# The gated delta rule of a two-layer decoder trunk: chunks of 128 tokens for chunks of 64

## The reference, cut to what matters

```python
def chunk_gated_delta_rule(q, k, v, g, beta):      # DN_CHUNK = 64
    q, k, v, g, beta = (chunks(t) for t in (q, k, v, g, beta))
    gc = jnp.cumsum(g, axis=-1)
    decay = jnp.exp(jnp.where(incl, gc[..., :, None] - gc[..., None, :], -jnp.inf))
    k_beta = k * beta[..., None]
    lower = jnp.where(strict, einsum(k_beta, k) * decay, 0.0)
    rhs = concatenate([v * beta[..., None], k_beta * jnp.exp(gc)[..., None]])
    u, w = triangular_solve(lower + eye(C), rhs)
    qk = einsum(q, k) * decay
    # scan over chunks, with a state of 128 x 128 per head:
    v_new = u - w @ state
    o = (q * exp(gc)) @ state + qk @ v_new
    state = state * exp(g_last) + (k * exp(g_last - gc)).T @ v_new
```

## Time and profile before

| | |
|---|---|
| median of 3 runs | 783.01 us (782.78 to 783.46) |
| the profiled execution | 782.49 us, span 780.5 us |
| TensorE, matmuls | 761.1 us busy, 98% of the span, 4506 records |
| VectorE | 581.5 us, 75% |
| ScalarE | 476.4 us, 61% |
| GpSimd | 169.9 us, 22% |
| memory reads | 122.06 MB, 158 GB/s over the span |

### The profile page before, as it was taken

How to read it: one execution, slowest core, us unless ns; L and a number is a source line. 1 busy time by engine, 2 the same in 40 slices (tenths; PEclk the granted TensorE clock), 3 DMA queues, 4 the chain that set the end, 5 groups by cost and what they waited for, 6 DMA issues and landing times.

```text
span 780.5 us, 12179 instructions
## 1 busy us (share of the span) xinstructions
PE 761.1 (98%) x4506; PEld 656.9 (84%) x4506; DVE 581.5 (75%) x846; ACT 476.4 (61%) x1073; POOL 169.9 (22%) x187
## 2 busy tenths in 40 slices
PE   7999999998999999999999999999999998999998
PEld 6999888887878788888899998888778787888886
DVE  6687878978788677666656886899795975867763
ACT  6869476677685744354457776765866657433451
POOL 1255105204031012321023511231030300126100
PEclk9999999999999999999999999999999999999999
DMA  8666455454645346455566563655356453455551
GB/s 247 207 194 200 159 142 155 136 162 135 165 136 187 109 135 189 140 184 176 149 196 182 158 193 104 182 153 171 111 153 171 136 186 112 145 179 162 172 179 55
DMA packets 73041, 124.97 MB, mean 160 GB/s; under 512 B 9757, under 2 KB 17047, under 8 KB 72983
## 3 DMA queue, kind: packets, MB, share of 16 engines
q1 hardware_dynamic: 72560, 124.13, 52.2%
q10 hardware_dynamic: 423, 0.06, 0.1%
HBM read 122.06 MB, written 1.05 MB: 158 GB/s over the span
## 4 chain that ended last, share of the span: by engine, by line
PE 76%; DVE 12%; ACT 7%; issue 3%; POOL 1%; DMA 0%; ACTq 0%; POOLq 0%
PE bank L787 19%; PE bank L789 19%; PE bank L788 19%; DVE w_lo L1464 3%; PE bank L769 3%; PE bank L771 3%; PE bank L770 3%; ACT at L1399 2%; ACT w_hi L1130 2%; PE bank L817 1%; PE bank L874 1%; ACT at L1196 1%; DVE gate L1818 1%; PE bank L927 1%; DVE at L1819 1%
## 5 line engine op out<-in xcount | busy, mean ns | idle before, releaser
L1464 DVE TENSOR_TENSOR w_lo<-raw,w_hi 128x1024 fp32r<-128x1024 f32 (+4 forms) x240 | 286.9, 1223 | 96.9 <-ACT w_hi L1130 94.5
L1130 ACT ACTIVATE w_hi<-raw 128x1024 fp32r<-128x1024 f32 (+4 forms) x239 | 235.8, 1017 | 96.1 <-PE bank L789 75.0
L787 PE MATMUL bank<-w_hi,hT 128*128 128x512 f32 (+2 forms) x704 | 277.6, 394 | 5.8 <-DVE mixed L1483 3.2
L789 PE MATMUL bank<-w_hi,hT 128*128 128x512 f32 (+2 forms) x704 | 271.0, 385 | 0.0
L788 PE MATMUL bank<-w_lo,hT 128*128 128x512 f32 (+2 forms) x704 | 270.6, 384 | 0.0
L787 PEld LDWEIGHTS bank<-w_hi,hT 128*128 128x128 f32 x704 | 132.9, 189 | 31.7 <-DVE mixed L1483 3.7
L789 PEld LDWEIGHTS bank<-w_hi,hT 128*128 128x128 f32 x704 | 132.7, 188 | 25.6
L788 PEld LDWEIGHTS bank<-w_lo,hT 128*128 128x128 f32 x704 | 133.0, 189 | 23.0
L1937 POOL TENSOR_TENSOR sm<-sm,tab 128x8 f32<-128x8 f32 (+3 forms) x46 | 55.9, 1216 | 208.0 <-ACT dn L1344 78.7
L769 PE MATMUL bank<-hT,w_hi 128*128 128x256 f32 x192 | 54.9, 286 | 0.0
L771 PE MATMUL bank<-hT,w_lo 128*128 128x256 f32 x192 | 54.3, 283 | 0.0
(11 more groups left out here) (228 smaller groups left out, 998.3 us busy)
## 6 DMA issues: line engine op xcount, KB each, us to landing
raw<-in_w_in SPq DMA_DIRECT2D x168, 512.0 KB, 4.3
raw<-in_w_branch SPq DMA_DIRECT2D x24, 512.0 KB, 4.5
raw<-in_w_out SPq DMA_DIRECT2D x16, 512.0 KB, 4.5
raw<-in_w_in SPq DMA_DIRECT2D x8, 384.0 KB, 5.3
raw<-in_w_in SPq DMA_DIRECT2D x8, 320.0 KB, 4.1
raw<-in_mla_w_kv_b SPq DMA_DIRECT2D x8, 256.0 KB, 3.0
raw<-in_mla_w_q_b SPq DMA_DIRECT2D x4, 384.0 KB, 3.4
xs<-in_x SPq DMA_DIRECT2D x2, 512.0 KB, 4.8
```

What stands on the lines that cost most here:

```text
L787: mm(o, src[0][:, a, tok], hi[:, k, :], start=starts and p == k == 0, stop=False)
L789: last = mm(o, src[1][:, a, tok], hi[:, k, :], start=False, stop=ends(u, p) and k == k1 - k0 - 1)
L1130: av(view(w_hi, q % SPLIT, k1 - k0, n), view(raw, q % RAW, k1 - k0, n), ACT.Copy).then_inc(hi_done, 1)
L1464: tt(view(w_lo, q % SPLIT, k1 - k0, n), view(raw, q % RAW, k1 - k0, n), view(w_hi, q % SPLIT, k1 - k0, n).bitcast(F32), ALU.subtract).then ...
```

## The change

The delta rule works in chunks of 128 tokens, one for each tile t, instead of 64.

- `dn_row` is made by transposes of the running sums instead of products, one step for each t, in banks 2 and 3; `rstd_row` is made by transposes too. `dn_gc` takes two products for four.
- `dn_kk` and `dn_qk` are whole 128x128 products, two steps each, in banks 4 and 7. `dn_kk` stands in unit 23, `dn_qk` in unit 24 behind `dn_kkE`, `dn_qkE` and `dn_G` in unit 25. `dn_bT` of v takes banks 2 and 3 instead of 7 and 6.
- The decay matrix `d_Dt` and what comes of it is 128x1024 instead of 128x512; VectorE evicts it in two steps.
- The inverse gets a second level: `dn_TX` also makes the transposed block of 32 (16 further records), then `dn_X64` and `dn_TX64` make the block of 64 under the diagonal. `dn_wide` has two more copies on ScalarE and two more memsets.
- `dn_u` is 8 whole products for 16 quarters, `dn_w` 4 for 16, and there is one `dn_ds`, one `dn_ws`, `dn_oc` of 8 whole products, and `dn_o` for t = 1 alone. The steps `dn_kd` (ScalarE) and `dn_dec` (GpSimd) are gone. `dn_bE` makes one product for each t instead of two.
- Some waits name both halves of a pair where they named the later one.

```diff
-    put(23, ("dn_decay",), ("dn_bT", 2, 0), ("dn_bT", 2, 1))
-    put(24, ("ahead",), ("dn_kkE",), ("dn_Uc",), ("dn_qkE",), ("dn_G",))
+    put(23, ("dn_decay",), ("dn_bT", 2, 0), ("dn_bT", 2, 1), ("dn_kk", 0), ("dn_kk", 1))
+    put(24, ("ahead",), ("dn_kkE", 0), ("dn_kkE", 1), ("dn_Uc",), ("dn_qk", 0), ("dn_qk", 1))
     put(38, ("dn_X",))
-    put(39, ("dn_kd",), ("dn_TX",))
-    put(40, ("dn_u", 0), ("dn_u", 1), ("dn_w",))
-    put(41, ("dn_ds", 0))
-    put(42, ("dn_ws", 1), ("dn_dec", 1))
-    put(43, ("dn_ds", 1))
-    put(44, ("dn_ws", 2), ("dn_dec", 2))
-    put(45, ("dn_ds", 2))
-    put(46, ("dn_ws", 3))
-    put(47, ("dn_oc", 0), ("dn_oc", 1), ("dn_o", 0), ("dn_o", 1))
-    put(48, ("dn_oss", 0), ("dn_oss", 1), ("dn_on",))
+    put(39, ("dn_TX",))
+    put(40, ("dn_X64",))
+    put(41, ("dn_TX64",))
+    put(42, ("dn_u", 0), ("dn_u", 1), ("dn_w",))
+    put(43, ("dn_ds",), ("dn_oc", 0))
+    put(44, ("dn_ws",))
+    put(45, ("dn_oc", 1), ("dn_o", 0), ("dn_o", 1))
+    put(47, ("dn_oss", 0), ("dn_oss", 1), ("dn_on",))
...
-            ("d_scale", g, 1), *([("dn_row",), ("dn_kk",), ("dn_qk",)] if g == 0 else []))
+            ("d_scale", g, 1), *([("dn_row", 0), ("dn_row", 1)] if g == 0 else []))
...
-    put(25, ("dn_H",))
+    put(25, ("dn_qkE", 0), ("dn_qkE", 1), ("dn_G",), ("dn_H",))
...
-    if k == "dn_bT" and a[0] == 2:
-        return [7 - a[1]]
...
+    if k == "dn_row":
+        return [2 + a[0]]
+    if k in ("dn_kk", "dn_qk"):
+        return [4 + 3 * a[0]]
+    if k in ("dn_X", "dn_X64", "dn_ws"):
         return [2]
+    if k in ("dn_TX", "dn_TX64", "dn_ds"):
         return [3]
+    if k == "dn_w":
         return [4]
...
+                four(step, layer, lambda o, h: tr(o, gcs[:, t, h:h + 1].broadcast_to([P, P]), ident))
...
+                four(step, layer, lambda o, h: mm(o, feature_tile(kT, t, h), feature_tile(kT, t, h), start=True, stop=True))
...
+                halves(step, layer, lambda o, n: mm(o[half_b, :], U_n[half_a, n, half_b], T_a[half_a, n, :], start=True, stop=True))
...
+                halves(step, layer, lambda o, n: mm(o[half_a, :], X_b[half_b, n, :], TT_n[half_b, n, half_b], start=True, stop=True))
```

More of the change, by code:

```diff
@@ L286, in banks @@
     if k == "dn_o":
-        return [5 + a[0]]
-    if k in ("dn_row", "dn_X"):
+        return [5] if a[0] else []
+    if k == "dn_row":
[3 more added lines that the diff above has]
+    if k in ("dn_X", "dn_X64", "dn_ws"):
         return [2]
-    if k == "dn_kk":
+    if k in ("dn_TX", "dn_TX64", "dn_ds"):
         return [3]
-    if k == "dn_qk":
+    if k == "dn_w":
         return [4]
[L294 to L301, removed]
     return []
@@ L364, in shape_tables @@
     put("ident", i == j)
[L365 to L368, removed]
+    put("tri", i <= j)
+    put("not_tri", np.where(i <= j, 0.0, NEG))
     row, column = np.divmod(np.arange(SUB * EACH)[None, :], EACH)
@@ L754, in unit @@
                 if t == 0 and what == "branch":
-                    pe.wait_ge(*taken(("yT", i // 2, 1), layer))
+                    for j in range(2):
+                        pe.wait_ge(*taken(("yT", i // 2, j), layer))
                 pair = "xT" if u < 2 else "mT" if what == "out" and i == 0 else None
@@ L937, in dn_gc @@
                 b = banks(step)[0]
-                for i, w in enumerate((const("tri"), const("same"), const("chunk")[:, 0:1].broadcast_to([P, P]),
-                                       const("chunk")[:, 1:2].broadcast_to([P, P]))):
+                for i, w in enumerate((const("tri"), const("one").broadcast_to([P, P]))):
                     last = mm(ps[b][:, i * NT * H:(i + 1) * NT * H], w, g_.rearrange("p t h -> p (t h)"), start=True, stop=True)
                 last.then_inc(bank_full[b], 1)
[L943 to L952, removed]
             def dn_row(step, layer):
-                blocks(step, layer, 0, lambda o, t, h, c, r: mm(o, g_[r, t, h:h + 1].broadcast_to([CH, CH]), const("tri")[r, r], start=True, stop=True))
+                t = step[1]
+                if t == 0:
+                    pe.wait_ge(*taken(("dn_gc",), layer))
+                four(step, layer, lambda o, h: tr(o, gcs[:, t, h:h + 1].broadcast_to([P, P]), ident))
             def rstd_row(step, layer):
@@ L1001, in dn_TX, with halves, dn_X64, dn_TX64 @@
                 pe.wait_ge(*free(step, layer))
-                across(b, lambda o, n, lo, hi: mm(o[lo, :], X[hi, n, :], d_Tt[hi, n, :], start=True, stop=True)).then_inc(bank_full[b], 1)
+                across(b, lambda o, n, lo, hi: mm(o[lo, :], X[hi, n, :], d_Tt[hi, n, :], start=True, stop=True))
+                hi = half_rows(0, 1)
+                for n in range(NT * H):
+                    last = mm(ps[b][hi, (NT * H + n) * SUB:(NT * H + n + 1) * SUB], d_Tt[hi, n, :], X[hi, n, :], start=True, stop=True)
+                last.then_inc(bank_full[b], 1)
+            def halves(step, layer, product):
+                b = banks(step)[0]
+                pe.wait_ge(*free(step, layer))
+                for n in range(NT * H):
+                    last = product(ps[b][:, n * CH:(n + 1) * CH], n)
+                last.then_inc(bank_full[b], 1)
+            def dn_X64(step, layer):
+                pe.wait_ge(*taken(("dn_TX",), layer))
+                pe.wait_ge(*after("scalar", ("dn_wide",), layer))
+                pe.wait_ge(*after("vector", ("dn_wide",), layer))
+                halves(step, layer, lambda o, n: mm(o[half_b, :], U_n[half_a, n, half_b], T_a[half_a, n, :], start=True, stop=True))
+            def dn_TX64(step, layer):
+                pe.wait_ge(*taken(("dn_X64",), layer))
+                halves(step, layer, lambda o, n: mm(o[half_a, :], X_b[half_b, n, :], TT_n[half_b, n, half_b], start=True, stop=True))
             def dn_u(step, layer):
@@ L1006, in dn_u @@
                 wait_taken(step, layer, ("dn_bT", 2, t))
[L1007 to L1015, removed]
@@ L1016, in dn_u @@
-                last.then_inc(bank_full[b], 1)
-            def dn_w(step, layer):
[L1020 to L1029, removed]
@@ L1031, in dn_ds @@
-            def dn_ds(step, layer):
[L1032 to L1040, removed]
-            def dn_ws(step, layer):
[L1043 to L1048, removed]
-                wait_taken(step, layer, ("dn_ds", c - 1))
-                four(step, layer, lambda o, h: mm(o, hd(wT, t, h), states[c][:, h * P:(h + 1) * P], start=True, stop=True))
+                pe.wait_ge(*taken(("dn_TX64",), layer))
@@ new lines, in dn_u @@
+                four(step, layer, lambda o, h: mm(o, d_TT[:, t, h, :], hd(vb, t, h), start=True, stop=True))
+            def dn_w(step, layer):
+                pe.wait_ge(*taken(("dn_TX64",), layer))
+                four(step, layer, lambda o, h: mm(o, hd(kbg, 1, h), d_TT[:, 1, h, :], start=True, stop=True))
+            def dn_ds(step, layer):
+                pe.wait_ge(*taken(("dn_u", 0), layer))
+                four(step, layer, lambda o, h: mm(o, hd(kdec, 0, h), hd(vnew, 0, h), start=True, stop=True))
@@ L1052, in dn_oc @@
+            def dn_ws(step, layer):
+                pe.wait_ge(*taken(("dn_w",), layer))
+                pe.wait_ge(*taken(("dn_u", 1), layer))
+                pe.wait_ge(*taken(("dn_ds",), layer))
+                four(step, layer, lambda o, h: mm(o, wT[:, h * P:(h + 1) * P], state[:, h * P:(h + 1) * P], start=True, stop=True))
             def dn_oc(step, layer):
                 t = step[1]
-                wait_taken(step, layer, ("dn_qk",))
-                pe.wait_ge(*taken(("dn_ws", 2 * t + 1), layer))
@@ L1057, in dn_oc @@
[L1057 to L1074 removed]
+                wait_taken(step, layer, ("dn_qk", t))
@@ L1076, in _ @@
+                pe.wait_ge(*taken(("dn_ws",) if t else ("dn_u", 0), layer))
+                four(step, layer, lambda o, h: mm(o, Aqk[:, t, h, :], hd(vnew, t, h), start=True, stop=True))
+            def dn_o(step, layer):
+                if step[1] == 0:
+                    return
+                pe.wait_ge(*taken(("dn_ds",), layer))
+                four(step, layer, lambda o, h: mm(o, feature_tile(qT, 1, h), state[:, h * P:(h + 1) * P], start=True, stop=True))
             parts = {"unit": unit, "xT": xT, "mT": mT, "yT": yT_step, "latT": latT, "tr": tr_step, "sc": sc, "pT": pT, "pv": pv,
@@ L1077, in _ @@
                      "dn_gc": dn_gc, "dn_row": dn_row, "rstd_row": rstd_row, "dn_bT": dn_bT, "dn_kk": dn_kk,
-                     "dn_qk": dn_qk, "dn_X": dn_X, "dn_TX": dn_TX, "dn_u": dn_u, "dn_w": dn_w, "dn_ds": dn_ds,
+                     "dn_qk": dn_qk, "dn_X": dn_X, "dn_TX": dn_TX, "dn_X64": dn_X64, "dn_TX64": dn_TX64, "dn_u": dn_u, "dn_w": dn_w, "dn_ds": dn_ds,
                      "dn_ws": dn_ws, "dn_oc": dn_oc, "dn_o": dn_o}
@@ L1151, in evict @@
                 elif what == "z" and i != A:
-                    act.wait_ge(*full(("yT", {C: A, B: C}[i], 1), layer))
+                    for j in range(2):
+                        act.wait_ge(*full(("yT", {C: A, B: C}[i], j), layer))
```

(34 more changed lines are left out.)

190 lines of the change are left out of this document (77 added, 113 removed).

## The result

The changed kernel takes 804.58 us (median of 4 runs, 803.33 to 806.59) against 782.89 for the kernel before (4 runs): ratio 1.0279, 95% interval 1.0255 to 1.0303. That is 21.7 slower; the forecast was 13 slower, and its range ended at 803. The profiled execution took 805.36, with a span of 803.6.

A forecast was written before the change was run, and what follows sets the result against it. TensorE's stream plus its waits bounds the kernel. Per layer +9.75 (waits with row, kk, qk), +1.1, +0.8 and -4.95 (remaining stream) make +6.7; twice +13.4, taken as +13: 796.0 against the median, range 791 to 800, wider 788 to 803.

The forecast's parts named there:

- rival (a): TensorE's clock falls to half pace after each of four stalls, 1.75 each: +7, 803; chance 0.16.
- The two new waits: TensorE waits at `dn_bT` behind `dn_row` (3.4 and 1.3) and at `dn_qk` behind `dn_kkE` (3.7): 8.45 a layer.
- The work moved into unit 25: `dn_qkE` and `dn_G` on VectorE lengthen TensorE's wait at L874 for GpSimd: +1.1 a layer, ends 0 and 3.5.
- `dn_wide`: ScalarE makes 6 copies instead of 4, ahead of w_hi and the branch eviction: +0.8 a layer, ends 0 and 0.8.
- The stream: TensorE's own matmuls and transposes, without the new waits: -3.65 a layer, 7 us faster with nothing else.
- `dn_X64` and `dn_TX64`: New TensorE steps, 16 records each on one array quarter: 1.0 each, +2.0 a layer, ends +1.0 and +3.5.
- TensorE's busy time: Sign in the changed profile: TensorE's busy time falls by about 7.
- rival (b): VectorE frees the banks early enough, leaving only the stream and `dn_wide`: -2.85 a layer, 777.3; chance 0.07.
- (c): Only one of the two new TensorE waits comes, say `dn_qk`'s 3.7: 787; chance 0.1.
- (d): Unit 25's lag passes in full (3.5) and the X64 steps cost their upper end: +8 in all, 804; chance 0.07.

The follow-up runs named there:

- The bank experiments: Changed kernel with transposes of v in banks 5 and 6: 794.25; separately, changed kernel with `dn_qk` in banks 2 and 3: 792.85.
- the run of 776.9: Kernel of 779.0 (both bank changes, `dn_G` and `dn_qkE` moved) with the two added `dn_wide` copies made by VectorE instead of ScalarE: 776.89.
- the wait alone: Kernel before, with TensorE made to wait behind unit 24 until VectorE has evicted `dn_kk`: 791.72 against 783.18.
- the filled kernel: Changed kernel with 8 idle products of 239 columns ahead of the first transpose of v and again ahead of `dn_qk`: 796.51.

## Why the prediction was wrong, step by step

**The step that failed** is rival (a), which was left at a chance of 0.16 and at nothing in the sum: the clock. Its own figure, 1.75 a stall and 7 in all, was near the 8.1 measured. It was set low because the granted clock reads full in all slices of the kernel before, and because no row showed a stall in midstream. But that row could not speak against it: behind the start no wait of that kernel is longer than 1.6, so the reading was of a state without the cause. The one place at which TensorE came out of idle time, the start, showed half pace, and it was put aside. The granted clock reads 1.00 there too, while the records take twice their time, so at the start the row doesn't show the pace. In its place the runs showed a clock at 0.50 behind the stalls. The Trainium skill, "TensorE: Matmul & The Clock Gate", section "Why this matters for your kernels", warns that an idle gap between bursts of matmuls takes the array back to half rate; the traces agree, at 0.50 behind waits of 3.51 and 3.67, and the runs with filled stalls bear it out. Forecast 796.0 plus 8.1 is 804.1; measured 804.6. The sum closes so well in part by chance, as the medians include the start, which differs by up to 1.4 us between the profiled executions.

**The two new waits** were right in mechanism, place and size: 3.4 and 1.3 forecast, 3.51 and 0.65 measured (with the stalls filled the second is 1.10; it is shorter here because the first transposes took longer at half pace), and 3.7 against 3.67. The bank experiments took each away from its place.

**The work moved into unit 25**, 1.1 a layer, came as 1.2, in another place: the wait L921 in unit 27 rose from 0.7 to 1.9, while GpSimd's stayed at 1.4, not 2.5.

**`dn_wide`**, 0.8 a layer, was right by accident of place: new waits of 1.3 and 1.0 for the gate's eviction, and 0.5 less in each wait for the branch eviction (L1451, before L1483). Where VectorE makes the copies, one of the two new waits is gone and the other is 0.8.

**The stream.** 16 records of `dn_kk` take 1.95 with the tail at full clock, 0.11 a record as taken. `dn_X64` and `dn_TX64` were put at 1.0; the timeline of the changed kernel has them at

```profile
287.39 1.14 PE L1007 MATMUL bank<-dn 64*64 64x64 f32 x16
...
295.15 1.14 PE L1011 MATMUL bank<-dn 64*64 64x64 f32 x16
```

with the tail, and 1.2 and 1.3 with the switch to and from the other shape. The upper end, 1.8 each, isn't reached. The Trainium skill, "TensorE: Matmul & The Clock Gate", section "Part 3: Packing small matmuls — row/col tiling", says that a weight load overlaps a running matmul only where the row groups differ; at 1.14 for 16 records on one row group, the trace doesn't bear out the 1.8 that the prediction read from that. TensorE's busy time was to fall by about 7; it rose by 4.5 at the lower clock, and at full clock behind the start (the run of 776.9, 755.8 us busy) it is 5.3 lower. The stream with `dn_wide` was priced at 777.3 in rival (b); with the long waits taken out it measured 779.0 and 776.9.

**Rival (b)**, faster, did not come, for the reason given; it became true once banks and order were changed. (c) did not come. (d), further waits, was not needed: 0.1 a layer of it at most.

## What to carry to other kernels

Where one engine's stream is the time, look up for every bank and buffer that a moved step takes who frees it and where that stands in the other engine's list: the waits here, with the clock that they brought down, cost several times what the shorter algorithm saves, and giving the steps other banks, with two steps moved on VectorE, turned 2.8% slower into 0.5 to 0.8% faster. In this kernel a stall of TensorE of 3.5 us cost up to its length plus about 2 us of half pace; price both, and don't read a full clock in a kernel without stalls as a sign that stalls are free. When a stall can't be removed, idle products in it are a cheap test, and here they brought back 8 of 22 us. And look where each profiled execution stands after the start, before comparing two of them.

## What the runs showed of the hardware

In the profiled executions, waits of 3.51, 3.60 and 5.60 us brought the granted clock to 0.50 for 6.8 us (149.5 to 156.3 behind the wait of 3.51; 157.5 to 164.3 with the wait alone), and it fell before the wait was over. The wait of 3.67 that came some 12 us behind such a wait brought it down for 3.4 us (166.6 to 170.0), 0.8 us after the wait had ended. The half pace cost 2.1 us a stall by itself (791.7 for 787.5) and 8.1 us for four stalls (804.6 for 796.5).

Shorter waits aren't safe, nor do they always bring the clock down: waits of 2.02 and 2.19 us in the start were followed by some 3.4 us at half, one of 1.96 in layer 1 of the filled kernel too, but the same wait in its layer 0 and the two of 1.94 in the changed kernel were not.

3.39 us of products that nothing reads, ahead of the same releases, kept the clock at 1.00 around the stalls in both layers of the changed kernel, and throughout the kernel before. And a delay of TensorE is partly given back: 3.8 us at unit 24 cost 2.2 a layer in the end.
